# Attention's transposes three steps behind the logits, and the weighing in odd steps

## The reference

```
proj = u @ w_in                      # [xp | q | k | v | gate_logits]
y_pool = causal_pool_mixer(xp, ...) @ w_branch_pool
z = (q @ k.T) * scale                # 8 heads of 64, strictly causal
beta = sigmoid(z)
A[t, s] = beta[t, s] * prod_{s<j<t} (1 - beta[t, j])     # stick breaking, no softmax
y_sb = (A @ v) @ w_branch_attn
g_pool, g_sb = split(sigmoid(gate_logits))
out = (g_pool * y_pool + g_sb * y_sb) @ w_out
```

## Time and profile before

| | |
|---|---|
| median of 3 runs | 1937.89 us |
| span of the profiled execution | 1937.1 us; the runs' median lies 0.8 us above it |
| TensorE matmul busy | 1923.7 us (99%) |
| DVE, ACT, POOL busy | 1338.3, 772.0, 136.9 us |
| the stage of the change | 882.7 to 1166.5 us of the span |

### The profile page before, as it was taken

One profiled execution on the slowest core, in us unless ns is written; L12 is line 12 of the kernel. 1 busy time (PEld: TensorE's weight loads), 2 busy tenths in 40 slices (PEclk: granted clock), 3 DMA queues, 4 the chain that ended last, 5 costly groups with the idle time before them and its releaser, 6 DMA issues.

```text
span 1937.1 us, 25171 instructions
## 1 busy us (share of the span) xinstructions
PE 1923.7 (99%) x9094; PEld 1607.4 (83%) x9094; DVE 1338.3 (69%) x1656; ACT 772.0 (40%) x1154; POOL 136.9 (7%) x218
## 2 busy tenths in 40 slices
PE   9999999999999999999999999999999999999998
PEld 9888888888888888888888888888888888888887
DVE  6987777775566667425777778789767776755655
ACT  7423232333434424214565652464323232324344
POOL 1000000000000100002333320010000000000002
PEclk9999999999999999999999999999999999999999
DMA  5456645468676503546645347643535454677665
GB/s 163 148 202 229 226 160 164 171 219 309 201 237 194 179 24 103 177 152 190 164 131 161 108 148 249 206 143 109 183 132 187 149 184 139 221 262 241 206 192 204
DMA packets 245092, 347.20 MB, mean 179 GB/s; under 512 B 16144, under 2 KB 150032, under 8 KB 240400
## 3 DMA queue, kind: packets, MB, share of 16 engines
q1 hardware_dynamic: 245008, 346.09, 54.9%
HBM read 232.79 MB, written 112.98 MB: 178 GB/s over the span
## 4 chain that ended last, share of the span: by engine, by line
PE 55%; DVE 2%; DMA 1%; issue 1%; ACT 1%; SPq 0%; POOL 0%; POOLq 0%; DVEq 0%; ACTq 0%
PE bank L1091 20%; PE bank L1188 12%; PE bank L1135 4%; PE bank L1137 4%; PE bank L1136 4%; PE bank L1047 2%; PE bank L1257 2%; PE bank L1285 2%; PE bank L1349 2%; DMA dn_lo_raw<-act_dram 1%; PE bank L1366 1%; PE bank L1365 1%; PE bank L1336 1%; PE bank L1334 1%; DVE tail_p L2471 0%
## 5 line engine op out<-in xcount | busy, mean ns | idle before, releaser
L1905 DVE TENSOR_TENSOR dn_lo<-dn_lo_raw,dn_hi 128x1024 fp32r<-128x1024 f32 x149 | 181.8, 1224 | 151.6 <-ACT dn_hi L1545 151.2
L1091 PE MATMUL bank<-hi_t,wa_hi 128*128 128x512 f32 x640 | 249.1, 389 | 0.2 <-issue 0.2
L1091 PE MATMUL bank<-hi_t,wa_lo 128*128 128x512 f32 x640 | 249.0, 389 | 0.0
L1091 PE MATMUL bank<-lo_t,wa_hi 128*128 128x512 f32 x640 | 249.0, 389 | 0.0
L1545 ACT ACTIVATE dn_hi<-dn_lo_raw 128x1024 fp32r<-128x1024 f32 x149 | 158.0, 1061 | 217.6 <-DMA dn_lo_raw<-act_dram 217.6
L1135 PE MATMUL bank<-dn_hi 128*128 128x512 f32 x596 | 232.7, 390 | 0.6 <-DVE dn_lo L1905 0.6
L1136 PE MATMUL bank<-dn_hi,dn_lo 128*128 128x512 f32 x596 | 231.9, 389 | 0.0
L1137 PE MATMUL bank<-dn_lo,dn_hi 128*128 128x512 f32 x596 | 231.9, 389 | 0.0
L1091 PE MATMUL bank<-hi_b,wa_hi 128*128 128x512 f32 x480 | 186.9, 389 | 0.5 <-DVE up L2029 0.5
L1091 PE MATMUL bank<-lo_b,wa_hi 128*128 128x512 f32 x480 | 186.8, 389 | 0.0
L1091 PE MATMUL bank<-hi_b,wa_lo 128*128 128x512 f32 x480 | 186.7, 389 | 0.0
(11 more groups left out here) (237 smaller groups left out, 3555.3 us busy)
## 6 DMA issues: line engine op xcount, KB each, us to landing
wa_lo_raw<-in_ffn_w_gate_up_dram SPq DMA_DIRECT2D x87, 512.0 KB, 5.0
dn_lo_raw<-act_dram SPq DMA_DIRECT2D x149, 256.0 KB, 4.3
act_dram<-g SPq DMA_DIRECT2D x44, 512.0 KB, 4.5
wd_t<-in_ffn_w_down_dram SPq DMA_DIRECT2D x44, 512.0 KB, 6.6
act_dram<-s_of SPq DMA_DIRECT2D x88, 256.0 KB, 6.5
wd_dram<-wd_t SPq DMA_DIRECT2D x22, 1024.0 KB, 6.0
dn_lo_raw<-wd_dram SPq DMA_DIRECT2D x85, 256.0 KB, 3.3
dn_lo_raw<-in_ffn_w_down_dram SPq DMA_DIRECT2D x64, 256.0 KB, 3.0
```

The costliest lines, as they stand in the source:

```text
L1091: last = nc.tensor.matmul(acc, lhs, rhs, start=n == 0 and i != 2 and i < 5, stop=n == 11, skip_group_check=True)
L1905: return nc.vector.tensor_tensor(dst, raw, hi.bitcast(f32), ALU.subtract)
```

## The change

`LAG` is new: the transposes of tile n stand in step n + 3 instead of n + 2, on TensorE, ACT and DVE. In a step of TensorE the weighing and the transposes come first, with no gate matmuls ahead of them (before, half of the step's gates stood ahead). The weighing of pair p moves from step 2p + 4 to step 2p + 5. On DVE the scan comes ahead of the low parts in every step; before, the low parts came first in steps that scan tiles 1, 5 and 3. `DRAIN` grows to 5, and `SHARE` has new numbers. SP's stores move with the weighing. No arithmetic is added or left out.

```
-DRAIN = 4
+DRAIN = 5
+LAG = 3
...
-SHARE = {7: 8, 6: 16, 1: 16, 0: 11, 5: 4, 4: 12, 3: 13, 2: 12}
+SHARE = {7: 7, 6: 10, 1: 16, 0: 4, 5: 4, 4: 5, 3: 11, 2: 9}
...                                              # SP
-                    if s == NA:
+                    if s == NA + 1:
                         move_o(NA // 2 - 2, 3, slice(0, HALF // 2))
-                    elif s == NA + 2:
+                    elif s == NA + 3:
                         move_o(NA // 2 - 1, 4, slice(HALF // 2, HALF))
-                    elif s >= 4 and s % 2 == 0:
-                        store_o((s - 4) // 2)
+                    elif s >= LAG + 2 and s % 2:
+                        store_o((s - LAG - 2) // 2)
...                                              # TensorE
-                cut = g0 + (g1 - g0) // 2
-                gate_parts(g0, cut)
-                if s >= 4 and s % 2 == 0:
-                    weigh((s - 4) // 2)
-                if 2 <= s < NA + 2:
-                    turn(s - 2)
+                if s >= LAG + 2 and s % 2:
+                    weigh((s - LAG - 2) // 2)
+                if LAG <= s < NA + LAG:
+                    turn(s - LAG)
                 if s < NA:
                     n = len(TILES[s]["chunks"])
+                    first = g0 + (g1 - g0) // 2 if s == 0 else g0
+                    gate_parts(g0, first)
                     for part in range(n):
-                        a0, a1 = (cut + (g1 - cut) * (part + k) // n for k in range(2))
+                        a0, a1 = (first + (g1 - first) * (part + k) // n for k in range(2))
                         logits(s, part)
                         gate_parts(a0, a1)
                 else:
-                    gate_parts(cut, g1)
+                    gate_parts(g0, g1)
...                                              # ACT: take_o and turned_hi by the same rule
...                                              # DVE
-                turned_first = 2 <= s <= NA and TILES[s - 1]["qt"] in (1, 5, 3)
-                if turned_first:
-                    turned_lo(s - 2)
                 if 1 <= s <= NA:
                     weigh_keys(s - 1)
-                if 2 <= s < NA + 2 and not turned_first:
-                    turned_lo(s - 2)
+                if LAG <= s < NA + LAG:
+                    turned_lo(s - LAG)
                 for j, piece in PIECES_AT[s]:
                     split_piece(j, piece)
```

More of the change, by code:

```diff
@@ L1856, in _ @@
             for s in range(NA + DRAIN):
[L1857 to L1860, removed]
+                if s >= LAG + 2 and s % 2:
+                    take_o((s - LAG - 2) // 2)
+                if LAG <= s < NA + LAG:
+                    turned_hi(s - LAG)
                 if s < NA:
```

## The result

The changed kernel takes 1947.43 us (median of 4 runs, 1945.39 to 1947.71) against 1938.03 before: 1.0046 times as long, 95% interval 1.0031 to 1.006. By the medians that is 9.4 us slower. The forecast was 1943.3 with a range up to 1946.8: the direction and the places were right, the time lies 0.6 us above the range.

What follows compares the result with a forecast made beforehand. TensorE was taken as the bound, busy 1923.7 of 1937.1 us. New waits of 8.6 us (4.0 + 0.5 + 1.6 + 2.0 + 0.5) less 3.2 old gave +5.4; with 0.8 from span to median, 1943.3 us, range 1939.8 to 1946.8.

Steps and rivals of the forecast that it cites:

- TensorE may not begin bank 31 until bank 29 is staged: End of the stage: bank 29 is staged only behind five outputs_hi, so TensorE waits 4.0 us before bank 31.
- The clock falls in the 4 us: Rival, chance 0.10: TensorE's clock drops in the wait before bank 31, adding about 1.7 us, to 1945.
- between span and median: Whole kernel: the median of the runs was taken to lie 0.8 us above the profiled span.
- Step 54, 1.6 us: Step 54: gate-weight pieces behind bank 24's stage delay DVE, stalling TensorE 1.6 us before the transposes of tile 53.
- The drain, 0.5: Drain before the last weighing ends: the last two weighings stall 0.25 us each, together 0.5.
- the start, 0.5: Start of the stage: the second tile's transposes still wait for the first tile's low parts, 0.5 us.
- The other steps, 2.0: Remaining steps: weighings wait for low parts when DVE is busy with a piece or product; four such meetings, 2.0 us.
- the waits for `a` go: Transposes: more lead time for the weighted keys should remove the 0.4 us lost on `a` twice.
- Hidden, with 1.7 us to spare: End of the stage: the outputs' loads, moved from step 61 to 63, do not lengthen the outputs' chain; 1.7 us spare.

Runs made afterwards that it cites:

- the old kernel at 718: The kernel before the change, with only the start of its last step moved from gate 720 to gate 718: 1944.44 us, ratio 1.0033.
- the kernel with the old shares: Changed kernel with last step at gate 720, step 54's pieces ahead of the stage on ACT, and the earlier SHARE: 1946.78 us, ratio 1.0044.
- the kernel with the old order on DVE: Changed kernel with last step at gate 720, step 54's pieces first on ACT, low parts ahead of scans of tiles 1, 5, 3: 1955.69 us.

## Why the prediction was wrong, step by step

- *"TensorE may not begin bank 31 until bank 29 is staged", 4.0 us.* Right in mechanism and size: 4.23. Removing it alone, and adding it alone to the kernel before, both show it.
- *"The clock falls in the 4 us", chance 0.10, price 1.7.* This is the step that failed. The prediction left the clock out of its sum and kept it as a rival; it fell in the profile and, by the mean granted clock, probably in all four runs, and cost 2.48. Without that the time is 1944.95, inside the range. The price too was small: what costs is the time under the low clock in which TensorE has work. Here 5.07 us of matmuls ran at 0.50 and lost about half of that; in the old kernel at 718 it was 3.3 us and 1.7 lost, the price that the prediction took from the program's start. (That the clock made that start slow is a reading: the earlier trace rows show slow matmuls there, not a low granted clock.)
  The other terms were close. The stage is 8.3 us longer; less 2.5 for the clock that is +5.8, where the sum had +5.4. The clock alone would have made 1945.8, still in the range. The rest, from there to 1947.43, is small pieces: 0.4 in the stage's waits, 0.5 outside the stage, and 0.6 between span and median, which the sum took as 0.8 and which is 1.4 for this profile.
  The page "TensorE: Matmul & The Clock Gate" of the Trainium skill, in "HAM oscillation — how this bites in real kernels", says that a wait between two groups of matmuls can throttle the engine, so that the next group starts at half the clock. The trace agrees: 0.50 behind a pause of 4.1 us, though in the old kernel at 718 the fall came only four matmuls into the next group. The prediction should have taken its own 4 us pause at that rule's word.
- *Step 54, 1.6 us.* Right: 1.79, and 1.6 came back when ACT's order was turned.
- *The drain, 0.5, and the start, 0.5.* The two weighings of the drain lost 0.34 and 0.24 (from start to start, less the 0.228 that a gate matmul takes anyway), the start 0.45.
- *The other steps, 2.0.* By the same rule four weighings lost 0.36, 0.90, 0.15 and 0.80, together 2.2; their kind, a low part behind DVE's own queue, was the one named. That the waits for `a` go was right.
- *"Hidden, with 1.7 us to spare"* for the outputs' loads: right, the chain took 8.25 us against 8.09 and was driven by DVE.

## What to carry to other kernels

Work moved by a plan of numbers also moves what the plan computes from them: see which event falls on which side of each boundary, before and after, and follow what the displaced one releases. A wait of TensorE can be paid twice, in the pause and in the matmuls behind it: here waits of 4.1, 3.9 and 1.8 us were. Filling such a wait with useless matmuls cost nothing here and saved the second payment; removing the wait saved both. And a longer lead for one operand wins nothing while another operand's queue sets the time: here order and shares gave 3.4 to 3.9 us with either lag.

## What was not expected of the hardware

With the clock low, a matmul of 512 columns started 0.427 us after the one before it, with the clock high 0.228, and the fall came inside the pause in one kernel (0.81 mean in its window) but about four matmuls behind a pause of 3.9 us in another; the price was 2.5 and 1.7 us. The length of a wait alone does not tell whether the clock falls: it fell behind one of 1.8 us in the kernel with the old shares, and stayed at 1.00 behind the 1.6 us of step 54 in the changed kernel and behind the longest wait, 2.2 us up to 1164.14, of the kernel with the old order on DVE:

```profile
1164.10:1170.00 5.90, 5.79 (x38) 4.96 (x39) 2.35 (x4) 1.48 (x3) 0.00 (x0) 1.00 1.05 345
```

DVE and GpSimd seem to hold each other up, and either can be the one that stands (spans of GpSimd are rough). The two pieces of step 54 took 2.04 us beside a GpSimd product of 1.29, and 1.28 without, about as the prediction had reckoned from the earlier trace rows. With the pieces moved ahead, the same GpSimd product ran beside a DVE scan that kept its 1.22 us; the GpSimd product took 2.11 instead, and DVE's next product 1.60, against 0.69 for the same product in the changed kernel.
